# Normed tiles behind norms 2, 3 and 5 one by one from tiles without factor and shift; stacks issued in the norm; last FFN's remainders on VectorE

## Chip, core and metric

One core of one Trainium2 chip runs the whole program. The metric is the device time in microseconds (us), the median of several runs. Engines by their short names: PE (TensorE), DVE (VectorE), ACT (ScalarE), POOL (GpSimd), SP (SyncE, here only a DMA queue).

## What is computed

512 tokens of width 1024, in float32, pass two blocks. Cut to its skeleton:

```python
# block 1
h = rms_norm(x, g_mix);  proj = h @ w_in          # RG-LRU and pooling branches, gates
x = x + merged @ w_out
h = rms_norm(x, g_ffn);  up = conv3(h @ w_up)     # norm 2
x = x + (gelu(up[:, :DF]) * up[:, DF:]) @ w_down
x = rms_norm(x, g_final)                          # norm "g"
# block 2; scale, shift and gate come from mod = silu(c) @ w_mod + b_mod
u = rms_norm(x, g1) * (1 + scale1) + shift1       # norm 3
xs, q, ckv, qi, ki, wi, ga, gb = split(u @ w_in)
y_ssm = s5(xs)                                    # state space branch
y_att = attention(top-128 of causal keys) @ w_attn_proj
x = x + gate1 * ((sig(ga) * y_ssm + sig(gb) * y_att) @ w_out)
u2 = rms_norm(x, g2) * (1 + scale2) + shift2      # norm 5
x = x + gate2 * ((silu(u2 @ w_gate) * (u2 @ w_up)) @ w_down)
return rms_norm(x, final_g)                       # norm 6
```

## The kernel before

**Layout.** Activations lie transposed: eight tiles of 128 channels by 512 tokens. A product of such a tile with weights is a row of "blocks", one block for each 128 by 128 piece of the weights, into one PSUM bank of eight. There are 1976 blocks, in a fixed order; eight blocks are a "unit" of 512 KB.

**Three matmuls a block.** Weights and activations are split into a rounded half (`hi`, fp32r) and a remainder (`lo`). `block` issues hi x hi (L702), lo x hi (L703) and hi x lo (L705), each 512 columns wide. A unit's way: SP loads it (L2435, four buffers `raw`), ACT rounds it (L1115, `whi`), and the remainder `wlo` comes either from ACT (L1124, the negative rounded copy) and a POOL DMA that adds `raw` to it (L2321), or, for the units in `BY_VECTOR`, from a DVE subtraction (L2068). Each stage has four buffers; unit u+4 can be rounded only when PE has done unit u, and loaded only when `wlo` of unit u is there. `weights(n)` in each engine's program moves a counter of blocks and does the units that come due, in that engine's order.

**Norms.** The squares are summed on PE (`sums`, one-column matmuls, L746), ACT takes the root, DVE the inverse, PE spreads it over 128 rows (`to_rows`, L790). DVE multiplies each tile by gain and factor (`nf`, L1556), ACT rounds it and adds the shift (L1151 or L1292), DVE makes the remainder (L1561 or L1544). `first` interleaves the next four tiles, block by block, so that each new normed tile feeds four blocks. Norm 2 already has its first four tiles from x times gain without the factor (`v2`), and DVE multiplies their results by the factor later (L2020). Norms 3 and 5 don't: PE finishes w_down or w_out_2, runs matmuls on unused data (`keep_warm`, L769), and waits for the normed tiles. Squares are summed in two parts there (tiles 0 to 6, and 7).

**Between norm 3 and norm 5** each engine is a set of generators: `d` (attention: index scores, top-128, softmax by pairs of heads), `s` (state space), `g` (gate products), `u` (GLU), `a` (attention projection). One string, `ORDER`, says whose next step follows, and all five engines walk the same string. A step of `g`, `u` or `a` is two blocks on PE. In `d`, a pair of heads has four steps of scores (tokens 3, 2, 1, 0 in quarters; L1004 on PE, DVE's minimum L2212, ACT's exponential L1424, and after the last DVE's reciprocal L2222 and product L2227), two of turning the probabilities (L1019), and one of the product with the values (L1029). `u` on DVE multiplies (L2252) and makes `mod_step`s (L1973): a row of w_mod times the condition, one column of scale, shift or gate each. PLACES gives the steps of `s` (inputs, turn, scan, output, each for four parts).

**Constants of the state space** are made during the first FFN: `CONSTS` says behind which j DVE makes them, `TURNS` behind which j PE turns them (L843) or makes the taps from them (L855), and SP stores them.

Of the kernel before, what the change touches and what calls it, by code (L numbers as in the profile page):

```python
# [319 lines left out]
def layout(k):  # L320
# [159 lines left out]
    for n in ("ssm_b", "ssm_c", "trig", "sbp", "sbt", "scs", "scp", "stt"):  # L480
        give(n)
    run([("uk",)], 2)
    for q in range(4):
        for n in TABS:
            run([(n, q)], TABS[n][1] // S)
# [183 lines left out]
def tensor_engine(k, T):  # L669
# [159 lines left out]
    for m in range(8):  # L829
        tile("w_out", m, range(8), "mg1", [2] if m == 7 else ())  # L830
# [3 lines left out]
    first(FIRST_UP, "v2", {(0, 3): lambda: sums([2], 7), (1, 3): lambda: to_rows(2)})  # L834
# [269 lines left out]
def scalar_engine(k, A):  # L1104
# [183 lines left out]
    root(2, 1024)
    weights(8)
    for m in range(8):  # L1290
        A.wait_ge(at("nf", 2, m), *freed("h2", m, "hi"))
# [1508 lines left out]
```

## Time and profile before

| | |
|---|---|
| median of 3 runs | 1485.59 us (1484.46 to 1486.53) |
| profiled execution | 1487.89 us, span 1486.6 us |
| mean granted clock of PE | 0.997 of full speed |
| PE busy | 98%, 6968 matmul records |
| DVE, ACT, POOL busy | 53%, 56%, 15% |
| DMA | 305.83 MB, mean 206 GB/s |
| to landing (median): raw, wlo, mod | 5.4, 6.3, 8.3 us |

A busy PE says little: the records of matmuls in a row overlap, so the table has 98% also where PE is not at its pace. What counts is the distance from one start to the next. Shares of DVE and ACT are averages over stages of very different load.

### The profile page before, as it was taken

To read this page: it belongs to the slowest core of one execution; us is meant where nothing else is said; L and a number is where in the kernel's file an instruction comes from. 1 tells how busy PE (TensorE), PEld (TensorE's weight loads), DVE (VectorE), ACT (ScalarE), POOL (GpSimd) and SP (SyncE) were. 2 spreads that over 40 slices of the span, in tenths; PEclk is the share of its full clock that TensorE was granted. 3 is DMA by queue.
4 is the path that set the end of the run, shared out by engine and by line. 5 is a ranking of instruction groups with operands and counts; after the bars stand their busy time and mean duration, and the time that the engine had idled before them with its cause. 6 is when DMAs were issued, how large, how long until landed. Compare 5 with 4: busy or idle time off the path is not lost.

```text
span 1486.6 us, 18211 instructions
## 1 busy us (share of the span) xinstructions
PE 1461.1 (98%) x6968; PEld 1191.0 (80%) x6968; DVE 783.0 (53%) x1463; ACT 836.7 (56%) x1122; POOL 222.9 (15%) x241
## 2 busy tenths in 40 slices
PE   9999999999999999999999999999989999999998
PEld 8887888888878778788878877776868888888886
DVE  7879754365595947465346678736663121110011
ACT  7698998755565646542333565686345444444441
POOL 1111111111111111100001421111111111111111
PEclk9999999999999999999999999999999999999999
DMA  9776887899999888783337667894677998888882
GB/s 267 193 188 169 200 200 190 212 322 309 248 265 265 224 207 217 186 267 123 108 105 274 204 171 172 205 277 161 197 192 201 251 218 202 184 190 197 198 184 85
DMA packets 94134, 305.83 MB, mean 206 GB/s; under 512 B 10896, under 2 KB 13200, under 8 KB 94048
## 3 DMA queue, kind: packets, MB, share of 16 engines
q0 software_dynamic: 29696, 108.08, 38.8%
q1 hardware_dynamic: 61104, 190.69, 37.4%
q10 hardware_dynamic: 3248, 5.90, 1.1%
q8 instruction: 55, 0.90, 0.2%
q14 instruction: 31, 0.25, 0.0%
HBM read 177.62 MB, written 17.83 MB: 131 GB/s over the span
## 4 chain that ended last, share of the span: by engine, by line
PE 84%; DVE 8%; ACT 4%; DMA 2%; issue 1%; POOL 0%; DVEq 0%; ACTq 0%
PE ps L702 26%; PE ps L705 26%; PE ps L703 26%; DMA tab<-pl_f 1%; DVE pl_f L1973 1%; PE ps L746 1%; ACT whi L1115 1%; PE ps L790 1%; DVE pl_r L1544 1%; ACT wlo L1124 1%; PE ps L1029 1%; DVE pl_f L2030 1%; DVE pl_f L2027 1%; PE ps L908 0%; ACT pl_f L1231 0%
## 5 line engine op out<-in xcount | busy, mean ns | idle before, releaser
L702 PE MATMUL ps<-pl_r,whi 128*128 128x512 f32 x1976 | 776.5, 393 | 9.4 <-DMA wlo<-raw 3.1
L705 PE MATMUL ps<-pl_r,whi 128*128 128x512 f32 x1976 | 770.2, 390 | 0.0
L703 PE MATMUL ps<-pl_r,wlo 128*128 128x512 f32 x1976 | 769.6, 389 | 0.0
L702 PEld LDWEIGHTS ps<-pl_r,whi 128*128 128x128 f32 x1976 | 371.2, 188 | 95.8 <-issue 12.5
L705 PEld LDWEIGHTS ps<-pl_r,whi 128*128 128x128 f32 x1976 | 371.2, 188 | 79.2 <-DVE pl_r L1561 0.9
L703 PEld LDWEIGHTS ps<-pl_r,wlo 128*128 128x128 f32 x1976 | 371.5, 188 | 75.8 <-issue 0.5
L1115 ACT ACTIVATE whi<-raw 128x1024 fp32r<-128x1024 f32 x246 | 259.1, 1053 | 191.3 <-PE ps L705 153.4
L2321 POOL DMA_DIRECT2D wlo<-raw x206 | 177.7, 864 | 969.2 <-ACT wlo L1124 946.6
L1124 ACT ACTIVATE wlo<-raw 128x1024 fp32r<-128x1024 f32 x206 | 215.4, 1046 | 0.0
L2293 DVE TENSOR_TENSOR pl_f<-ps,pl_f 128x512 f32<-128x512 f32 x22 | 15.2, 691 | 170.6 <-PE ps L705 170.6
L1544 DVE TENSOR_TENSOR pl_r<-pl_f,pl_r 128x512 fp32r<-128x512 f32 x112 | 77.5, 692 | 31.2 <-ACT pl_r L1144 21.7
L2068 DVE TENSOR_TENSOR wlo<-raw,whi 128x1024 fp32r<-128x1024 f32 x39 | 51.4, 1328 | 50.7 <-ACT whi L1115 50.6
L1144 ACT ACTIVATE pl_r<-pl_f 128x512 fp32r<-128x512 f32 x34 | 21.5, 632 | 92.0 <-DVE pl_f L2293 77.0
L2270 DVE SCALAR_TENSOR_TENSOR pl_f<-ps,sml,pl_f 128x512 f32<-128x512 f32 x16 | 12.0, 749 | 116.3 <-PE ps L705 116.3
L1303 ACT ACTIVATE pl_f<-ps,vec 128x512 f32<-128x512 f32 x44 | 33.9, 775 | 55.1 <-PE ps L705 53.3
L1134 ACT ACTIVATE pl_f<-pl_f 128x512 f32<-128x512 f32 x37 | 22.9, 627 | 69.7 <-DVE pl_f L2270 49.8
L1973 DVE CUSTOM_DVE_ANT_0 pl_f<-pl_f,pl_f 128x1024 f32<-128x1024 f32 x48 | 57.9, 1218 | 0.0
L2027 DVE SCALAR_TENSOR_TENSOR pl_f<-ps,vec,pl_f 128x511 f32<-128x511 f32 x44 | 32.7, 744 | 13.2 <-ACT pl_f L1303 13.1
L1497 ACT ACTIVATE pl_f<-ps 128x512 f32<-128x512 f32 x22 | 13.1, 597 | 41.3 <-PE ps L705 41.3
L2030 DVE SCALAR_TENSOR_TENSOR pl_f<-ps,vec,pl_f 128x511 f32<-128x511 f32 x44 | 33.0, 750 | 1.6
L1680 DVE SCALAR_TENSOR_TENSOR pl_f<-pl_f,pl_f 128x512 f32<-128x512 f32 x20 | 12.9, 689 | 34.4 <-ACT pl_f L1243 34.4
L1914 DVE TENSOR_TENSOR pl_f<-pl_f,lams 128x640 f32<-128x640 f32 x4 | 3.3, 826 | 51.3 <-DMA tab<-pl_f 51.3
(270 smaller groups left out, 1095.2 us busy)
## 6 DMA issues: line engine op xcount, KB each, us to landing
raw<-in_w SPq DMA_DIRECT2D x245, 512.0 KB, 5.4
wlo<-raw POOLq DMA_DIRECT2D x206, 512.0 KB, 6.3
pl_f<-in_mod SPq DMA_DIRECT2D x48, 512.0 KB, 8.3
pl_f<-tab SPq DMA_DIRECT2D x12, 512.0 KB, 5.6
xs<-pl_f SPq DMA_DIRECT2D x16, 256.0 KB, 6.1
tab<-pl_f SPq DMA_DIRECT2D x8, 512.0 KB, 6.7
pl_f<-xs SPq DMA_DIRECT2D x16, 256.0 KB, 5.3
spill<-pl_f ACTq DMA_DIRECT2D x16, 256.0 KB, 3.5
```

What stands on the lines that cost most here:

```text
L702: matmul(out, wh, sr(pair, kk, "hi"), start=start, stop=False)
L703: matmul(out, wl, sr(pair, kk, "hi"), start=False, stop=False)
L705: mm = matmul(out, wh, sr(pair, kk, "lo"), start=False, stop=stop)
L1115: act(k.whi[:, u % NHI, :], k.raw[:, u % NRAW, :], ACT.Copy).then_inc(*k.w_hi.tick(("w_hi", u)))
L1124: act(k.wlo[:, u % NLO, :], k.raw[:, u % NRAW, :], ACT.Copy, scale=-1.0).then_inc(*k.w_neg.tick(("w_neg", u)))
L1303: act(sb("up", j), ps("w_up", j), ACT.Identity, bias=vc("conv_f_b", j), scale=vc("conv_f_w", 44 + j)).then_inc(*done.tick(("up_tap", j)))
L1544: tt(sr(pair, m, "lo"), src, sr(pair, m, "hi").bitcast(F32), ALU.subtract).then_inc(*done.tick((pair, m, "lo"), *freed_by))
L1973: V.eng.tensor_tensor_reduce(r, r, sb(*c), 1.0, 0.0, ALU.mult, ALU.add, sm("mod", u)).then_inc(*done.tick(("mod_used", u), *([mod_home(u)] ...
L2027: stt(f[:, 1:S], b[:, 0:S - 1], vc("conv_f_w", j), f[:, 1:S], ALU.mult, ALU.add).then_inc(*done.tick())
L2030: stt(f[:, 0:S - 1], b[:, 1:S], vc("conv_f_w", 88 + j), f[:, 0:S - 1], ALU.mult, ALU.add).then_inc(*done.tick(("up", j), ("w_up", j)))
L2068: tt(k.wlo[:, u % NLO, :], k.raw[:, u % NRAW, :], k.whi[:, u % NHI, :].bitcast(F32), ALU.subtract).then_inc(*done.tick(("w_lo", u)))
L2321: P.eng.dma_start(k.wlo[:, u % NLO, :].bitcast(F32), k.raw[:, u % NRAW, :], accum_op=ALU.add).then_inc(*k.w_lo[u % NLO].tick(("w_lo", u)))
```

## The change

1. **Norms 3 and 5** get what norm 2 has: `v3` and `v5`, tiles of x times gain without factor and shift, feed the first four tiles. The factor is multiplied in afterwards (`scaled`), and the shift, which passes through the weights, is added as a column for each tile: DVE sums the raw weights times the shift (`shift_part`, 8 operations of 128 columns for each of the units 133 to 136 and 181 to 184), PE sums over the rows (`shift_cols`), and ACT adds the column as a bias. SP must wait for `shift_used` before it loads over these units.
2. **The first four tiles** behind norms 2, 3 and 5 come one by one (`in_turn`), not interleaved. The squares are summed once (`sums_once`), and ACT copies the factor's rows to SBUF (`row`). keep_warm goes from norms 3 and 5. w_out_2 interleaves two tiles, not four.
3. **Remainders**: units 138 and 139 move from DVE to ACT and POOL; 185 and 188 to 246 (the last FFN) move from ACT and POOL to DVE (`subtracted`).
4. **Mod steps**: 13 in `u`, not 4; 3 ahead of w_out_2, none in it (12 before). SP's loads of them move with them.
5. **TURNS**: the taps of parts 0, 1 and 2 move from j = 8, 14, 20 to 9, 15, 21.
6. **ORDER and PLACES** are new. SP issues the copies that stack xs (L2580) for parts 1 and 2 in the norm, not at the steps of `s`.

```diff
-BY_VECTOR = [*range(115, 146), *range(169, 177)]
+BY_VECTOR = [*range(115, 138), *range(140, 146), *range(169, 177), 185, *range(188, NUNIT)]
 ORDER = (
-    "dsgggsggsgsgdgsdgggsggdgsgsgdsdgssssgdggggggggdsgddgggggsgdgdgsugdgggddgggdsdduuuduggduddg"
-    "gdgdgggggddudgggdgdgduugdgggugdugdguduuudddduuuudddduuaudduduuuudduddddduuuddddaaaaagauaaa"
+    "dgsgsggssgsgdggdsgdggdgggsgsgsgsgssddgsgggsggggdgudsgggdsgdggdgugddggdguggdddugugduggugdg"
+    "gdgdgddgggdsgggguddgddddggggugdguuduuudddduddduuuudduuuddddduuuuauddudddudduuddddagaauaaaaaa"
     "auaaaaa"
 )
-PLACES = [("b", 0), ("t", 0), ("c", 0), ("b", 1), ("t", 1), ("b", 2), ("t", 2), ("o", 0),
-          ("c", 2), ("c", 1), ("b", 3), ("t", 3), ("c", 3), ("o", 1), ("o", 2), ("o", 3)]
+PLACES = [("b", 0), ("t", 0), ("c", 0), ("b", 1), ("t", 1), ("o", 0), ("b", 2), ("c", 1),
+          ("t", 2), ("c", 2), ("b", 3), ("o", 1), ("t", 3), ("c", 3), ("o", 2), ("o", 3)]
-TURNS = {6: ("b", 0), 8: ("c", 0), 12: ("b", 1), 14: ("c", 1), 18: ("b", 2), 20: ("c", 2),
+TURNS = {6: ("b", 0), 9: ("c", 0), 12: ("b", 1), 15: ("c", 1), 18: ("b", 2), 21: ("c", 2),
...
@@ tensor_engine @@
+    def in_turn(tiles, pair, between):
+        for n, t in enumerate(tiles):
+            out = take(*t)
+            for kk in range(8):
+                block(t, kk, pair, out, kk == 0, kk == 7)
+                for step in between.get((n, kk), ()):
+                    step()
...
-    keep_warm(480, 256)
-    sums([3, "g"], 7)
-    keep_warm(256)
-    to_rows(3)
-    keep_warm(480, 256)
-    first(FIRST_IN_2, "u")
-    to_rows("g")
+    in_turn(FIRST_IN_2, "v3", {(0, 6): [lambda: sums_once(3, "g")],
+                               (1, 2): [lambda: to_rows(3), lambda: shift_cols(0), lambda: to_rows("g")]})
...
-    first([("w_out_2", m) for m in range(4)], "mg2")
+    first([("w_out_2", m) for m in range(2)], "mg2")
...
+    in_turn(FIRST_FFN_2, "v5", {(0, 7): [lambda: sums_once(5)],
+                                (1, 3): [lambda: to_rows(5), lambda: shift_cols(1)]})
@@ scalar_engine @@
+    def normed(n, pair, shift=None, between={}):
+        weights(16)
+        A.wait_ge(at("rows", n), *freed("row", n))
+        act(sb("row", n), ps("rows", n), ACT.Copy).then_inc(*done.tick(("row", n), ("rows", n)))
...
     root(5, 1024)
+    weights(8)
+    rounded_weights(units.ahead())
     normed(5, "h5", lambda m: sm("mod", 24 + m))
@@ vector_engine @@
+    def shift_part(i, part):
+        u = SHIFT_UNITS[4 * i + part]
+        r = sb("shift", i)[:, 128 * part:128 * part + 128]
+        V.wait_ge(at("raw", u))
+        for q in range(8):
+            col, raw = sm("mod", 24 * i + q), k.raw[:, u % NRAW, 128 * q:128 * q + 128]
...
-            if m > 3:
-                mod_step()
+            mod_step((0, 0, 1, 2, 3, 2, 3, 2)[m])
...
     inverse(5)
+    subtracted(185)
...
     for j in range(22):
+        if j > 2:
+            subtracted(184 + 2 * j)
...
+        if j == 1:
+            subtracted(188)
+        elif j > 1:
+            subtracted(185 + 2 * j)
         rest("act2", j, sb("f2", j), ("f2", j))
@@ sync_engine @@
+            if u - NRAW in SHIFT_UNITS:
+                Q.wait_ge(at("shift_used", u - NRAW))
...
-    weights(32)
-
+    weights(24)
     stack(0)
+    weights(8)
+    stack(1)
+    stack(2)
```

## Rows read from the trace of the kernel before

**Rows 1.** The page's busy time of each engine, with its share of the span.
```profile
PE 1461.1 (98%) x6968; PEld 1191.0 (80%) x6968; DVE 783.0 (53%) x1463; ACT 836.7 (56%) x1122; POOL 222.9 (15%) x241
```

**Rows 2.** PE in order of time, w_down: start, length, line, tiles [idle before].
```profile
754.51 0.39 PE L703 MATMUL ps<-pl_r,wlo 128*128 128x512 f32 x1
754.74 0.39 PE L705 MATMUL ps<-pl_r,whi 128*128 128x512 f32 x1
```

**Rows 3.** PE in order of time, in w_out and in the first FFN.
```profile
379.11 0.95 PE L746 MATMUL ps<-cst,pl_f 128*128 128x1 f32 x8
...
428.39 0.47 PE L702 MATMUL ps<-pl_r,whi 128*128 128x512 f32 x1 [1.93 <-DVE pl_f L1872]
```

**Rows 4.** DVE's groups by line and shape: busy us, mean ns | idle before.
```profile
L1544 DVE TENSOR_TENSOR pl_r<-pl_f,pl_r 128x512 fp32r<-128x512 f32 x112 | 77.5, 692 | 31.2 <-ACT pl_r L1144 21.7 <-ACT pl_r L1292 6.3 <-ACT pl_r L1193 0.8
...
L2068 DVE TENSOR_TENSOR wlo<-raw,whi 128x1024 fp32r<-128x1024 f32 x39 | 51.4, 1328 | 50.7 <-ACT whi L1115 50.6
...
L1556 DVE SCALAR_TENSOR_TENSOR pl_f<-pl_f,sml,ps 128x512 f32<-128x512 f32 x16 | 11.9, 743 | 3.3 <-PE ps L790 3.3
...
L1942 DVE TENSOR_TENSOR pl_f<-pl_f,sml 128x128 f32<-128x128 f32 x4 | 1.2, 293 | 0.1
```

**Rows 5.** PE's waits by line: us in total, times, longest.
```profile
PE ps L855 <- DVE pl_f L1922: 3.3, 3, 1.8
```

**Rows 6.** PE in order of time, norm 3.
```profile
754.97 1.84 PE L746 MATMUL ps<-cst,pl_f 128*128 128x1 f32 x16
756.67 0.49 PE L702 MATMUL ps<-pl_r,whi 128*128 128x512 f32 x1
...
788.59 1.05 PE L790 MATMUL ps<-cst,sml 128*128 128x128 f32 x8
789.40 0.48 PE L702 MATMUL ps<-pl_r,whi 128*128 128x512 f32 x1
```

**Rows 7.** Stretches: length, busy time (records) of five engines, PE clock, DMA share, GB/s.
```profile
754.97:789.40 34.43, 33.50 (x158) 26.39 (x157) 17.97 (x26) 13.20 (x20) 0.00 (x0) 0.95 0.35 124
...
1027.60:1030.90 3.30, 3.30 (x10) 2.53 (x9) 1.34 (x9) 3.28 (x13) 0.00 (x0) 0.50 0.33 120
```

**Rows 8.** PE in order of time, w_out_2 and norm 5.
```profile
1099.57 0.47 PE L702 MATMUL ps<-pl_r,whi 128*128 128x512 f32 x1 [1.48 <-DMA wlo<-raw]
...
1104.22 0.39 PE L705 MATMUL ps<-pl_r,whi 128*128 128x512 f32 x1
...
1114.49 0.47 PE L702 MATMUL ps<-pl_r,whi 128*128 128x512 f32 x1 [0.52 <-ACT pl_r L1151]
```

**Rows 9.** POOL and SP's queue in order of time, w_out_2.
```profile
1095.02 0.86 POOL L2321 DMA_DIRECT2D wlo<-raw  x1 [15.43 <-ACT wlo L1124]
...
1099.45 9.66 SPq L2435 DMA_DIRECT2D raw<-in_w  x3
```

**Rows 10.** DVE and POOL in order of time, a step of `u`.
```profile
1002.76 1.22 DVE L1973 CUSTOM_DVE_ANT_0 pl_f<-pl_f,pl_f 128x1024 f32<-128x1024 f32 x1
...
1003.92 2.29 DVE L2068 TENSOR_TENSOR wlo<-raw,whi 128x1024 fp32r<-128x1024 f32 x1
...
1002.94 2.18 POOL L2406 TENSOR_TENSOR pl_f<-pl_f,pl_f 128x512 f32<-128x512 f32 x1 [8.58 <-DVE pl_f L2252]
```

**Rows 11.** PE, ACT and DVE in order of time, heads 2 and 3 (pair 1).
```profile
984.92 2.43 PE L1004 MATMUL ps<-pl_f,pl_f 64*128 64x512 f32 x16
...
995.24 0.82 PE L1019 MATMUL ps<-cst,pl_f 128*128 128x128 f32 x3 [0.38 <-ACT pl_f L1461]
...
990.81 0.39 ACT L1424 ACTIVATE pl_f<-pl_f,sml 128x128 f32<-128x128 f32 x1
...
991.63 2.46 DVE L2227 TENSOR_SCALAR pl_f<-pl_f,sml 128x128 f32<-128x128 f32 x8
```

**Rows 12.** PE in order of time, behind the scores of pair 3.
```profile
1026.90 0.47 PE L702 MATMUL ps<-pl_r,whi 128*128 128x512 f32 x1 [0.69 <-DVE sml L2212]
...
1030.36 0.63 PE L702 MATMUL ps<-pl_r,whi 128*128 128x512 f32 x1
```

More of the change, by code:

```diff
@@ L475, in layout @@
     for m in range(8):
+        if m == 5:
+            for n in ("ssm_b", "ssm_c", "trig", "sbp", "sbt", "scs", "scp", "stt"):
+                give(n)
+            for q in range(8):
+                pair("v3", q)
+            take("shift", 0)
         squares("g", m)
@@ L479, in layout @@
         give_pair("act1", j)
[L480 to L485, printed above, removed]
+    for n in TABS:
+        run([(n, 0)], TABS[n][1] // S)
     give("sq", "g", 0)
@@ L492, in layout @@
         take("st", q)
+    give("shift", 0)
+    run([("uk",)], 2)
+    for n in TABS:
+        run([(n, 1)], TABS[n][1] // S)
+    for m in range(8):
+        give_pair("v3", m)
+    give("row", 3)
+    for q in range(2, 4):
+        for n in TABS:
+            run([(n, q)], TABS[n][1] // S)
     for m in range(8):
@@ L644, in layout @@
     assert not [c for c in "dsgau" if next(steps[c], "end") != "end"]
+    take("shift", 1)
+    for m in range(8):
+        pair("v5", m)
     for m in range(8):
@@ L650, in layout @@
     normed(5, "h5")
+    for m in range(8):
+        give_pair("v5", m)
+    give("row", 5)
+    give("shift", 1)
     for j in range(22):
@@ L761, in sums_of, with shift_cols, sums_once @@
         give("sums", n)
+    def shift_cols(i):
+        b = take("shift_cols", i)
+        T.wait_ge(at("shift_sum", i))
+        for n in range(4):
+            mm = matmul(b[:, n:n + 1], sb("shift", i)[:, 128 * n:128 * n + 128], k.ones[:, 0:1],
+                        start=n == 0, stop=n == 3)
+        mm.then_inc(*done.tick(("shift_cols", i), ("shift", i)))
+        give("shift_cols", i)
+    def sums_once(*norms):
+        b = take("sums", norms[0])
+        for i, n in enumerate(norms):
+            T.wait_ge(at("sq_part", n, 0))
+            for t in range(4):
+                mm = matmul(b[:, 4 * i + t:4 * i + t + 1], sb("sq", n, 0)[:, 128 * t:128 * t + 128],
+                            k.ones[:, 0:1], start=i == t == 0, stop=(i, t) == (len(norms) - 1, 3))
+            mm.then_inc(*done.tick(("sums", norms[0]) if n == norms[-1] else None, ("sq", n, 0)))
+        give("sums", norms[0])
     def keep_warm(*widths):
@@ L829, in tensor_engine @@
     for m in range(8):
[L830 removed]
+        tile("w_out", m, range(8), "mg1")
     done.release(*[("mg1", i, h) for i in range(8) for h in ("hi", "lo")])
[L834 removed]
+    in_turn(FIRST_UP, "v2", {(0, 5): [lambda: sums_once(2)], (1, 2): [lambda: to_rows(2)]})
     done.release(*[("v2", i, h) for i in range(8) for h in ("hi", "lo")])
@@ L1284, in scalar_engine @@
             *done.tick(("v2", m, "hi")))
+    root(2, 1024)
     rounded_weights(units.ahead())
[L1288 to L1291, printed above, removed]
-        act(sr("h2", m, "hi"), sb("nf", 2, m), ACT.Copy).then_inc(*done.tick(("h2", m, "hi")))
-        if m % 2:
-            weights(4)
-    A.wait_ge(at("rows", 2), *freed("row", 2))
-    act(sb("row", 2), ps("rows", 2), ACT.Copy).then_inc(*done.tick(("row", 2)))
-    weights(8)
+    normed(2, "h2")
     def up(j):
@@ L1551, in halves, with normed, factored @@
         rest(pair, m, src, *freed_by)
-    def normed(n, pair, xname, made, gain, shift=None):
+    def normed(n, pair, xname, made, gain, shift=None, between={}):
+        def factored(m):
+            V.wait_ge(at("row", n), at(*made, m), *freed("nf", n, m))
+            stt(sb("nf", n, m), sb(xname, m), gain(m), sb("row", n), ALU.mult,
+                ALU.mult).then_inc(*done.tick(("nf", n, m)))
+        factored(0)
         for m in range(8):
-            V.wait_ge(at("rows", n), at(*made, m), *freed("nf", n, m))
-            stt(sb("nf", n, m), sb(xname, m), gain(m), ps("rows", n), ALU.mult,
-                ALU.mult).then_inc(
-                    *done.tick(("nf", n, m), *([("rows", n)] if m == 7 and n != 2 else [])))
+            if m < 7:
+                factored(m + 1)
             if shift:
@@ L2059, in vector_engine, with subtracted @@
     units.blocks = BLK_DOWN
+    def subtracted(u):
+        V.wait_ge(at("w_hi", u))
+        if u - NLO not in BY_VECTOR:
+            V.wait_ge(at("unit", u - NLO))
+        tt(k.wlo[:, u % NLO, :], k.raw[:, u % NRAW, :], k.whi[:, u % NHI, :].bitcast(F32),
+           ALU.subtract).then_inc(*done.tick(("w_lo", u)))
     def weights(n):
@@ L2588, in s5 @@
         for step, q in PLACES:
-            if step == "b" and q < 3:
-                stack(q + 1)
+            if (step, q) == ("b", 0):
+                stack(3)
             if step == "t" and q in (0, 1):
```

229 lines of the change are left out of this document (145 added, 84 removed).

## The prediction, made before the change was run

> **What bounds the kernel now.** I read the page's busy line first. PE is busy 98% of the span [rows 1], but busy time says little here, as the records of neighbouring matmuls overlap. So I went to PE's own order of time. Two neighbouring starts in a plain stretch lie 0.23 us apart (754.51, 754.74) [rows 2]; that is the pace of a block's three matmuls, 0.68 us a block. The 5928 block matmuls at this pace are 1344 us of the 1486.6. The chip is bound by PE's stream, and a change is worth what it takes out of that stream (small matmuls, waits) less what it puts in. Work of DVE, ACT, POOL or the queues counts only where PE comes to wait for it. So I looked for PE's breaks near each edit, then for what each edit makes late.
>
> **Norm 2.** (T is the end of PE's w_out, and in norms 3 and 5 that of w_down and w_out_2.) One of two groups of eight one-column matmul records goes: 0.95 us of records at 379.11 [rows 3], of which the last overlaps the next block, so 0.8 us of PE's time. DVE now multiplies by a copy of the factor made by ACT, which comes behind ACT's weights(16), so its start slips from T+7.3 to about T+10; eight tiles of two DVE operations (0.74 and 0.69 to 0.75) [rows 4] are 12 us, with 2.8 us of scaling between them. They end near T+25; PE has done the four tiles at 32 x 0.68 + 1.6 = 23.4 and needs the eighth h2 at T+28. Hidden, with 3 us of cover. Behind it PE loses 1.9 us at 428.39 [rows 3], named after DVE, though ACT and the raw loads had fallen behind. DVE's scaling ends some 2 us earlier than before, and SP's loads with it: between nothing and the whole 1.9 comes back; I take 1.0, the middle.
>
> **TURNS.** The small tap matmuls (L855) of the first three parts go one j later, 16 blocks or 10.9 us. The three waits there sum to 3.3 us [rows 5], none over 1.8, so all go: 3.3 us. Below, SP's store of tt moves too and could hold raw loads (gain 0). The store waited for PE's turn before as well, so I take 3.3.
>
> **Norm 3.** From the first small matmul at 754.97 to the block behind the "g" rows at 789.40 are 34.4 us [rows 6, 7]. In it lie 99 matmuls of blocks, 22.4 us. What else must stay: the sums once, 754.97 to 756.67, 1.7; rows 3 and rows g, each 788.59 to 789.40, 0.8; and, new, shift_cols, eight one-column records as at 379.11, 0.8 [rows 3, 6]. Sum 22.4 + 1.7 + 0.8 + 0.8 + 0.8 = 26.5: 7.9 us less. Will it be covered? w_down ends at T; DVE adds the last tile to 1.7 (it first has w_lo 134 and 135, 1.3 us each [rows 4]), squares, makes v3 7 by 3.3, adds both sums by 4.7; PE asks for them at 7 x 0.68 = 4.8. A tie, 0.1 us. The normed u takes 12 us plus 2.5 of scaling from T+11 plus about 2 behind ACT's weights: T+28. PE asks for u 7 at 26.5 + 4.8 = T+31. The 32 DVE operations of shift_part(0) (128 columns; 0.29 us for the nearest such row [rows 4]) are 9 us in the last w_down tiles, where DVE has 15 us a tile. SP's new wait for shift_used has only raw loads behind it, and comes after w_lo of the same unit, which they waited for anyway: nothing. Stacks on SP: stack 1 and 2 wait for ACT's xs 2 near T+28 with the next raw loads behind them; those feed PE only at T+58. Nothing. I take 7.8.
>
> **Norm 5.** 1104.45 to 1114.49 holds one block and 9.4 us else [rows 8]: a wait for DVE's gain2, keep-warm, sums, rows. Kept: sums, rows, new shift_cols, 3 x 0.8 = 2.4. So 7.0 less. The wait before it for w_lo (1.48, 1099.57) came from ACT standing behind DVE's mod steps; these are moved, so 1.5 less. New: ACT makes unit 183 only after the root, and PE needs it 16 blocks and 2.4 us behind T, at 13.3. ACT has it at 8.7; its DMA took 4.4 us from 1095.02 to SP's next load at 1099.45 [rows 9], so 13.3 at best; one of 6.3 (the page's median) makes PE wait 1.9. h5 7, behind unit 185 on DVE, comes near 29.5, wanted at 29. I take 0.8 for both: 7.7 gained; bounds 4 and 8.5. That the shared work of DVE and POOL grows could cost more: a subtraction next to a POOL tensor operation took 2.29 us, against 1.33 in the mean of all 39 [rows 4, 10]. [...]
>
> **Last FFN.** 60 subtractions of 1.3 us [rows 4] go to DVE, which has 5.3 us of work in each 10.9 us pair of tiles. subtracted(185+2j) stands behind f2 j, which waits for PE; it is needed 10.9 us after that and done 2.3 us after. Cover 8.6 us. PE is at its pace there now, so freeing ACT and the POOL queue gives nothing: 0. If the cover failed, each of 60 units would cost.
>
> **ORDER.** This decides. Each letter takes a generator one step, so I laid both strings against the steps of the generators ("d": 27 steps, then for each pair of heads four scores, two turns, one product; "g", "u" and "a" put two blocks each, 1.36 us, between). The old string gives PE's order as the trace has it, to the block: in pair 1 four scores, "uuuu", both turns. The new one has 58 "d" for 55 steps, and those of pairs 1 to 3 stand where the spare ones have pushed them. Pair 0 keeps twelve blocks between scores and turns. Pair 1 has "ddd" (scores 3, 2, 1), "u", "ddd" (score 0 and both turns). Pair 2 has score 3, "uuu", "ddddd" (scores 2, 1, 0 and both turns). Pair 3 has score 3, "u", "ddd" (scores 2, 1, 0), "u", "dd" (both turns). A turn (L1019) needs all four queries' parts: DVE's minimum, ACT's exponentials, DVE's reciprocal and product. For pair 1 now: scores from 984.92, the last exponential over at 991.2, products 991.63 to 994.1 [rows 11]. That is 9.2 us from the first score. Before, 24 block matmuls stood in it. Now the scores (2.4) and two blocks (1.4) do: the 20 turn records (2.1) would be done at 5.9 and are at 9.7. Stall 3.8 us. Pair 2: from score 2, pair 1's 9.2 less the two widest exponentials, 1.7, plus another table load for the sigmoid between, 1.3: 8.8, and some 0.6 for DVE's three mod steps (1.22 each) [rows 10] and its subtraction; without waiting 3.5. Stall 5.9. Pair 3: u6.3 puts a multiply and three mod steps, 4.4 us, on DVE between score 3 and score 2; chain 11 against 4.9. Stall 6.1. Together 15.8 us. PE idles 4 to 6 us three times. The granted clock was 0.95 in norm 3, where PE stood, instead of 1.00, and 0.50, 1.2 GHz, behind the waits that end at 1026.90, where a block's record took 0.63 us, not 0.39 [rows 2, 7, 12]. That lasted 3.4 us and cost 1.5. Two or three of those: 3.8. By the Trainium skill, "TensorE: Matmul & The Clock Gate", section "What's actually happening", an idle stretch brings the half clock and activity releases it; here that would be three, 4.5, where the rows alone leave two open. Against this the waits of the old order in pairs 1 to 3 go, as those at 995.24 and 1026.90: by the starts of PE's records, against the same records unhindered, 1.8, 1.4 and 1.3 us, and the half clock's 1.5 [rows 11, 12], some 6.0. Net 15.8 + 3.8 - 6.0 = +13.6. Bounds: 0 (DVE and ACT turn out to be early enough and the old waits stay) to +27 (each chain 3 us longer, by subtractions of 2.29). I take 13.6.
>
> **Sum.** -0.8 - 1.0 - 3.3 - 7.8 - 7.7 + 13.6 = -7.0. The profiled execution took 1487.9 us (span 1486.6, 1.3 around it); its successor should take 1480.9. The median of the runs is 2.3 lower than the profiled one, so 1478.5.
>
> **Rivals.** (A) The turns do not stall: another reading of ORDER, or chains that are shorter without the work between. For it: ACT and DVE are less loaded there than PE. Against: the two chains that I followed took 9.2 us (pair 1, from the first score) and 7.4 (pair 2, from the last score). Then -20.6: 1465. Chance 0.22. (B) The norms' streams starve: DVE makes remainders, squares and normed tiles in turn with ACT, and PE, that now comes without a pause, waits for v3, unit 183, u and h5, 2 us at each of three places: 1484.5. For it are the tie at T+4.8 and the h5 of 29.5 against 29. Chance 0.14. (C) Slower: the softmax chains of pairs 1 to 3 grow. It decides when they lose more than 20.6 net, that is 9 us each with a half clock behind each (27 + 4.5 - 6 = 25.5 net, 1490.5). The place is DVE in pairs 2 and 3, with three mod steps and subtractions of 2.29. Chance 0.11. (D) The parts cancel and nothing is to be seen, 1485.6: 0.06. The forecast has 0.47, and its own range is 1473 to 1483.
>
> **How the numbers follow.** 0.2% is 3 us, about what a measurement of this kernel can tell from no change. Faster: A, nearly all of the forecast, a third of B, 0.73. Same: two thirds of B and D, 0.14. Slower: C and bits, 0.13. The range leaves out C's upper half and the end of A: 1463 to 1488.
>
> **What would show it.** PE's order of time: blocks without a break from w_down into w_in_2 and from w_out_2 into the FFN, no keep-warm, about 26.5 us for the same norm 3 work; no L855 wait; then at the turns of pairs 1, 2 and 3 waits for DVE's product of 3 to 6 us each, with the granted clock low behind them. No such waits, and I am wrong by 13 us on the fast side. A wait for w_lo 12 to 15 us after w_out_2 would be unit 183. Waits in the last FFN, at any j, would mean that DVE has no cover.

## The result, and where the time went

The changed kernel took 1470.32 us (median of 4 runs, 1467.47 to 1471.86) against 1486.06 of the kernel before (4 runs, 1484.46 to 1490.65). The ratio is 0.9877, with a 95% interval of 0.9861 to 0.9894. That is 15.7 us less; the prediction had 7.0 less (1478.5, range 1463 to 1488). The profiled execution took 1471.86 us, its span 1470.2 against 1486.6.

First a mistake that the reader must know of. The ORDER quoted above in the diff, and laid out in the prediction, is miscopied. The first line of it lacks one "g" (behind "ssdd" comes "gsgggg", not "gsggg"), which shifts nothing in the attention. The second has two "d" too many. These are the two lines of the kernel that ran:

```
"dgsgsggssgsgdggdsgdggdgggsgsgsgsgssddgsggggsggggdgudsgggdsgdggdgugddggdguggdddugugduggugdg"
"gdgdgddgggdsgggguddgddddggggugdguuduuudduddduuuudduuuddddduuuuauddudddudduuddddagaauaaaaaa"
```

They hold 56 "d", not 58. Laid against the generators again they give pair 1 score 3, two blocks, scores 2, 1 and 0, eight blocks, both turns; pair 2 four scores, twelve blocks, both turns; pair 3 scores 3 and 2, two blocks, scores 1 and 0, four blocks, both turns. So each chain keeps four to twelve blocks of cover, where the prediction had none or two.

The busy line and two groups of the page after (cf. [rows 1, 4]): POOL's DMAs finish 148 remainders, DVE makes 97.

```profile
PE 1450.7 (99%) x6932; PEld 1188.3 (81%) x6932; DVE 886.9 (60%) x1613; ACT 787.0 (54%) x1080; POOL 173.6 (12%) x183
...
L2461 POOL DMA_DIRECT2D wlo<-raw x148 | 127.9, 864 | 839.1 <-ACT wlo L1173 698.4
L2162 DVE TENSOR_TENSOR wlo<-raw,whi 128x1024 fp32r<-128x1024 f32 x97 | 120.1, 1242 | 93.0 <-ACT whi L1164 92.9
```

PE's blocks are the same 1976 in both kernels, so I counted the first matmul of each block (L702 before, L725 after) and took the differences of their starts. Each stretch begins and ends at such a start:

| stretch (blocks) | before | after | difference | forecast |
|---|---|---|---|---|
| start to w_out (to 520) | 368.91 | 371.82 | +2.9 | 0 |
| w_out, norm 2, its stall (520 to 600) | 59.48 | 56.28 | -3.2 | -1.8 |
| rest of the first FFN (600 to 1050) | 317.73 | 317.29 | -0.4 | -3.3 |
| norm 3 (1050 to 1100) | 46.11 | 38.56 | -7.6 | -7.8 |
| gated part, attention (1100 to 1430) | 298.89 | 298.17 | -0.7 | +13.6 |
| w_out_2, norm 5 (1430 to 1500) | 59.10 | 51.69 | -7.4 | -7.7 |
| last FFN (1500 to 1975) | 323.81 | 323.81 | 0.0 | 0 |

The differences sum to -16.4, as the spans do. The largest miss by far is in one row, the attention's. No run below takes the edits of norms 2, 3 and 5 out again: those rows rest on the same blocks timed in both kernels.

**Norm 3**, PE in order of time; it answers to [rows 6].

```profile
759.67 1.84 PE L813 MATMUL ps<-cst,pl_f 128*128 128x1 f32 x16
...
764.23 1.05 PE L845 MATMUL ps<-cst,sml 128*128 128x128 f32 x8
765.12 0.95 PE L802 MATMUL ps<-cst,pl_f 128*128 128x1 f32 x8
765.94 1.14 PE L845 MATMUL ps<-cst,sml 128*128 128x128 f32 x8
766.83 0.48 PE L725 MATMUL ps<-pl_r,whi 128*128 128x512 f32 x1
...
786.67 0.39 PE L725 MATMUL ps<-pl_r,whi 128*128 128x512 f32 x1
```

The sums of both norms stand once between blocks. Rows 3, shift_cols and rows g stand together, 764.23 to 766.83. The window from the first sum to the block behind the same 33 blocks, with the columns of [rows 7]:

```profile
759.67:786.67 27.00, 27.00 (x141) 23.07 (x139) 20.92 (x34) 14.88 (x22) 1.72 (x2) 1.00 0.72 213
```

It is 27.0 us against the 34.4 of [rows 7] and the 26.5 of the forecast; the granted clock is 1.00 in it, where it was 0.95.

**Norm 5**: PE in order of time, cf. [rows 8].

```profile
1099.92 0.50 PE L725 MATMUL ps<-pl_r,whi 128*128 128x512 f32 x1 [0.64 <-ACT pl_r L1197]
...
1101.05 0.95 PE L813 MATMUL ps<-cst,pl_f 128*128 128x1 f32 x8
```

PE waits 0.64 us for the v5 that ACT makes from the last tile. Nothing else ends a wait here, unit 183 and h5 included: in place of 9.4 us there are the sums, the rows and shift_cols, and this wait.

**Attention**: PE in order of time, scores (L1056) and turns (L1071) of pairs 1, 2 and 3, cf. [rows 11, 12].

```profile
973.40 1.13 PE L1056 MATMUL ps<-pl_f,pl_f 64*128 64x512 f32 x4
...
976.05 1.57 PE L1056 MATMUL ps<-pl_f,pl_f 64*128 64x384 f32 x12
...
984.03 3.07 PE L1071 MATMUL ps<-cst,pl_f 128*128 128x128 f32 x20 [0.74 <-DVE pl_f L2348]
...
993.43 3.30 PE L1056 MATMUL ps<-pl_f,pl_f 64*128 64x512 f32 x16
...
1005.57 3.06 PE L1071 MATMUL ps<-cst,pl_f 128*128 128x128 f32 x20 [0.44 <-DVE pl_f L2348]
...
1012.25 1.77 PE L1056 MATMUL ps<-pl_f,pl_f 64*128 64x512 f32 x8
...
1017.17 2.21 PE L1056 MATMUL ps<-pl_f,pl_f 64*128 64x256 f32 x8 [1.55 <-DVE pl_r L1614]
```

Turn waits of 0.74 and 0.44 us, none at pair 3. The largest loss is a new one: score 1 of pair 3 waits 1.55 us, and a stretch at 1.2 GHz stands behind it (granted clock 0.50 from 1019.3 to 1022.4).

**First FFN**: the stall of [rows 3] at 428.39 is gone and so are the three waits of [rows 5], but a new stall stands at 503.21: PE, then the window behind it.

```profile
503.21 0.47 PE L725 MATMUL ps<-pl_r,whi 128*128 128x512 f32 x1 [2.06 <-DVE pl_f L2127]
...
505.00 0.63 PE L728 MATMUL ps<-pl_r,whi 128*128 128x512 f32 x1
```

```profile
503.70:507.00 3.30, 3.30 (x9) 2.61 (x9) 3.23 (x5) 3.13 (x10) 0.86 (x1) 0.51 1.06 235
```

The page names DVE L2127 for this wait, but DVE's operation is due on each tile. What was late is a unit's weights: SP's queue, then ACT.

```profile
472.88 0.33 SPq L2577 DMA_DIRECT2D raw<-in_w  x1
473.30 0.91 SPq L2648 DMA_DIRECT2D tab<-pl_f  x1
491.70 0.33 SPq L2625 DMA_DIRECT2D pl_f<-in_mod  x1
492.13 11.30 SPq L2577 DMA_DIRECT2D raw<-in_w  x4
```

```profile
499.29 1.06 ACT L1164 ACTIVATE whi<-raw 128x1024 fp32r<-128x1024 f32 x1 [5.49 <-DMA raw<-in_w]
```

SP is through with a store at 474.2. Its next instruction is the load of modulation weights (`mod`, L2625), which must wait until DVE has used an older tile; it goes at 491.70. Four raw loads stand behind it in the program. ACT, which makes whi from them, stands still for 5.49 us until 499.29. The stall is 2.2 us by the starts and the half clock (0.51) costs 1.4 more: what TURNS gave is gone again.

The hold is not new. In the kernel before the same load goes at 490.37, behind a store of 473.11, and PE waits 0.50 us at the same block. Counted from block 600 it goes 62.0 us on there and 63.6 in the changed kernel. What delays it by 1.6 us is not shown; with the same code it varies, as E1 shows.

### The profile page after: what moved, and what is told of

Same layout as the page of the kernel before. It is cut to its first block, busy times and chain, and to the rows that moved or that the text cites. A ratio compares the mean times of both kernels' runs of the same rounds, so it can differ in the third digit from the quotient of the medians.

```text
span 1470.2 us, 18182 instructions
## 1 busy us (share of the span) xinstructions
PE 1450.7 (99%) x6932; PEld 1188.3 (81%) x6932; DVE 886.9 (60%) x1613; ACT 787.0 (54%) x1080; POOL 173.6 (12%) x183
## 4 chain that ended last, share of the span: by engine, by line
PE 86%; DVE 5%; ACT 5%; DMA 2%; issue 1%; POOL 0%; DVEq 0%; ACTq 0%
PE ps L725 27%; PE ps L728 27%; PE ps L726 27%; DVE pl_f L2050 1%; DMA wlo<-raw 1%; ACT whi L1164 1%; ACT wlo L1173 1%; ACT pl_f L1287 1%; PE ps L1071 1%; PE ps L845 1%; DMA tab<-pl_f 1%; PE ps L960 0%; PE ps L979 0%; DVE pl_f L2073 0%; PE ps L834 0%
## 5 line engine op out<-in xcount | busy, mean ns | idle before, releaser
L725 PE MATMUL ps<-pl_r,whi 128*128 128x512 f32 x1976 | 777.5, 393 | 8.4 <-DMA wlo<-raw 2.7
L725 PEld LDWEIGHTS ps<-pl_r,whi 128*128 128x128 f32 x1976 | 372.2, 188 | 91.9 <-issue 8.8
L2461 POOL DMA_DIRECT2D wlo<-raw x148 | 127.9, 864 | 839.1 <-ACT wlo L1173 698.4
L2162 DVE TENSOR_TENSOR wlo<-raw,whi 128x1024 fp32r<-128x1024 f32 x97 | 120.1, 1242 | 93.0 <-ACT whi L1164 92.9
L1173 ACT ACTIVATE wlo<-raw 128x1024 fp32r<-128x1024 f32 x148 | 154.8, 1046 | 0.0
L2050 DVE CUSTOM_DVE_ANT_0 pl_f<-pl_f,pl_f 128x1024 f32<-128x1024 f32 x48 | 63.1, 1331 | 3.8 <-ACT pl_f L1325 3.8
L1599 DVE TENSOR_TENSOR pl_f<-pl_f,pl_f 128x512 f32<-128x512 f32 x34 | 23.6, 693 | 19.8 <-ACT pl_f L1183 19.0
L2127 DVE SCALAR_TENSOR_TENSOR pl_f<-ps,vec,pl_f 128x511 f32<-128x511 f32 x44 | 33.0, 750 | 1.5
L1757 DVE SCALAR_TENSOR_TENSOR pl_f<-pl_f,pl_f 128x512 f32<-128x512 f32 x20 | 12.9, 689 | 34.4 <-ACT pl_f L1299 34.4
```

The source lines that it names most:

```text
L725: matmul(out, wh, sr(pair, kk, "hi"), start=start, stop=False)
L1173: act(k.wlo[:, u % NLO, :], k.raw[:, u % NRAW, :], ACT.Copy, scale=-1.0).then_inc(*k.w_neg.tick(("w_neg", u)))
L2050: V.eng.tensor_tensor_reduce(r, r, sb(*c), 1.0, 0.0, ALU.mult, ALU.add, sm("mod", u)).then_inc(*done.tick(("mod_used", u), *([mod_home(u)] ...
L2127: stt(f[:, 0:S - 1], b[:, 1:S], vc("conv_f_w", 88 + j), f[:, 0:S - 1], ALU.mult, ALU.add).then_inc(*done.tick(("up", j), ("w_up", j)))
L2162: tt(k.wlo[:, u % NLO, :], k.raw[:, u % NRAW, :], k.whi[:, u % NHI, :].bitcast(F32), ALU.subtract).then_inc(*done.tick(("w_lo", u)))
L2461: P.eng.dma_start(k.wlo[:, u % NLO, :].bitcast(F32), k.raw[:, u % NRAW, :], accum_op=ALU.add).then_inc(*k.w_lo[u % NLO].tick(("w_lo", u)))
```

## The experiments

All times are medians. The kernel before, timed beside each group of experiments, stood at 1488.3 (E1 to E4), 1487.9 (E5 to E8), 1489.0 (E9 and E10) and 1488.9 us (E11), so ratios say more than times. Differences between kernels of under 3 us are not settled by either; for them the text goes by the stretches, and each stretch is of one execution. Stretches are by counted blocks, as above.

**E1, the changed kernel again.**

> The changed kernel once more, unchanged. In the profiled execution of it the first 32 block matmul groups start 2.7 us later, against the kernel before, than they should with the same code, and the loss stays. Theory: this differs from execution to execution (a wait and a stretch of 1.2 GHz at 19 to 25 us), so here it can be gone or of another size, and the time is 1470 give or take 3. Rival: it belongs to the changed kernel (its constants, its loads); then the same wait of 1.8 us at 19.4 stands here too, and in each of the kernels below, whose first 300 us are the same.

Measured: 1468.85 us (4 runs, 1465.99 to 1473.80), ratio 0.9877 [0.9855, 0.9899]. Block 32 starts at 32.67 us, as in the kernel before (32.86), not at 35.57. Over the twelve profiled executions of this study's kernels it starts between 32.6 and 35.6, with the same code. So the +2.9 of the table is the execution, not the kernel. The stall at 500 differs in the same way: here it is 0.5 us, without a half clock (blocks 600 to 900: 209.96 us, in the first execution 213.57); the held load goes 61.3 us behind block 600, not 63.6. Behind block 950 the two executions agree to 0.2 us.

**E2, the order as the prediction read it.**

```diff
-... "ggggugdguuduuudduddduuuudduuuddddd" ...
+... "ggggugdguuduuudddduddduuuudduuuddddd" ...
```

> The changed kernel with the order as the prediction read it: two more d behind the 130th letter, so that scores and softmax turns of pairs 1 to 3 stand as close as the prediction had them. Theory (the prices of the step were right, only the string was misread): waits of about 3.8, 5.9 and 6.1 us at the turns of pairs 1, 2 and 3 and 3.8 us of 1.2 GHz, together 19.6, where the changed kernel has about 5.5 of such losses: 14 us above it, 1484. Rival (DVE and ACT catch up while PE stands, so that the chains are shorter than summed): 1.5 to 3 us at each turn, 3 to 6 us above it, 1473 to 1476.

Measured: 1486.52 us (10 runs), ratio 0.9993 [0.9981, 1.0004]: 17.7 us above the changed kernel (E1), where the theory had 14 and the rival 3 to 6, and all the gain is gone. PE at pairs 1 to 3:

```profile
972.77 2.25 PE L1056 MATMUL ps<-pl_f,pl_f 64*128 64x512 f32 x12
976.53 0.49 PE L1056 MATMUL ps<-pl_f,pl_f 64*128 64x128 f32 x4
...
981.36 4.33 PE L1071 MATMUL ps<-cst,pl_f 128*128 128x128 f32 x20 [4.34 <-DVE pl_f L2348]
...
993.42 1.13 PE L1056 MATMUL ps<-pl_f,pl_f 64*128 64x512 f32 x4
...
998.78 1.57 PE L1056 MATMUL ps<-pl_f,pl_f 64*128 64x384 f32 x12
...
1006.90 4.78 PE L1071 MATMUL ps<-cst,pl_f 128*128 128x128 f32 x20 [6.56 <-DVE pl_f L2348]
...
1022.49 1.13 PE L1056 MATMUL ps<-pl_f,pl_f 64*128 64x512 f32 x4
...
1025.13 1.57 PE L1056 MATMUL ps<-pl_f,pl_f 64*128 64x384 f32 x12
...
1032.24 0.77 PE L725 MATMUL ps<-pl_r,whi 128*128 128x512 f32 x1 [5.54 <-DVE sml L2333]
...
1035.96 4.23 PE L1071 MATMUL ps<-cst,pl_f 128*128 128x128 f32 x19 [0.82 <-DVE pl_f L2348]
```

The turns of pair 1 wait 4.34 us (forecast 3.8), those of pair 2 6.56 (5.9); in pair 3 the block ahead of the turns waits 5.54 and they another 0.82, 6.4 together (6.1). The granted clock is 0.50 at all three: from 981.7 to 985.1, 1005.6 to 1012.4 and 1029.5 to 1039.7. The stretch from block 1100 to 1400 takes 295.15 us, 16.7 more than before; the forecast for it was +13.6. It is 17.4 more than in the changed kernel, and PE's waits (17.3 and 2.9 us) explain 14.4 of that. The other 3.0 and the 1.5 that the half clock costs the changed kernel make an estimate of 4.5 us for the half clock here, where the step had 3.8. DVE in pair 2:

```profile
996.84 1.22 DVE L2050 CUSTOM_DVE_ANT_0 pl_f<-pl_f,pl_f 128x1024 f32<-128x1024 f32 x1
...
997.98 2.30 DVE L2050 CUSTOM_DVE_ANT_0 pl_f<-pl_f,pl_f 128x1024 f32<-128x1024 f32 x1
...
1001.35 1.21 DVE L2162 TENSOR_TENSOR wlo<-raw,whi 128x1024 fp32r<-128x1024 f32 x1
...
1006.47 2.46 DVE L2348 TENSOR_SCALAR pl_f<-pl_f,sml 128x128 f32<-128x128 f32 x8
```

Three mod steps and a subtraction, 996.84 to 1002.5, stand between the minima of score 3 and those of score 2; only then come the other minima, exponentials, reciprocal and the products at 1006.47. The turns start at 1006.90, while the products still run. So the stalls are what the prediction made them, to 0.7 us; it is the string that was read wrongly. The agreement is in part luck. Counted to the end of the products the chains are longer than it had them (pair 2 from score 2: 998.78 to 1008.93, 10.2 us for 9.4), and the turns do not wait for that end.

**E3, ORDER and PLACES of the kernel before.**

```diff
-    "dgsgsggssgsgdggdsg" ... (ORDER and PLACES as changed)
+    "dsgggsggsgsgdgsdgg" ... (ORDER and PLACES as before)
```

> The changed kernel with ORDER and PLACES of the kernel before. Theory: the two orders cost the same within a microsecond (by the starts of the block matmuls the attention stage took 0.7 us less in the changed kernel), 1471. Rival: the new order pays for what the new norm 3 makes late (stacks, u, table loads); with the old one PE waits in the first 100 us behind norm 3, some 3 to 6 us, 1474 to 1476.

Measured: 1473.56 us, ratio 0.9903 [0.9887, 0.992], 3 to 5 us above the changed kernel. The theory falls by the time and the rival by the place. No new wait stands behind norm 3: blocks 1100 to 1250 take the 137.7 us that they took before (the new order 136.0). The loss comes later, in the attention.

```profile
985.33 3.08 PE L1071 MATMUL ps<-cst,pl_f 128*128 128x128 f32 x20 [1.07 <-DVE pl_f L2348]
...
1008.50 3.06 PE L1071 MATMUL ps<-cst,pl_f 128*128 128x128 f32 x20 [1.87 <-DVE pl_f L2348]
...
1020.08 1.09 PE L1056 MATMUL ps<-pl_f,pl_f 64*128 64x128 f32 x4 [2.71 <-DVE pl_r L1614]
...
1021.87 0.49 PE L725 MATMUL ps<-pl_r,whi 128*128 128x512 f32 x1 [0.69 <-DVE sml L2333]
```

Waits of 1.07, 1.87, 2.71 and 0.69 us: blocks 1100 to 1400 take 282.17 us, with the new order 277.77, in the kernel before 278.49. So beside the other edits the old order is 3.7 us dearer than it was, and the new one takes 4.4 off.

**E4, SP's loads of modulation weights later.**

```diff
-        if 2 <= j < 8:
+        if 3 <= j < 9:
             load_mod()
```

> The changed kernel with SP's six loads of modulation weights in the first FFN one j later (3 <= j < 9 instead of 2 <= j < 8). In the changed kernel PE waits 2.2 us at 500.8 and runs 1.6 us long at 1.2 GHz behind it; the last of those loads stood in SP's queue from 474 to 491.7 until DVE had used an older tile, with four raw loads behind it. Theory: the raw loads come about 10 us earlier and the whole goes, 3.8 us below the changed kernel, 1466.5. Rival (the raw loads are late because the transfers themselves are slow there, or DVE's own work is what PE waits for): the wait stays, same time.

Measured: 1467.25 us, ratio 0.9865 [0.985, 0.988]. Blocks 600 to 900 take 209.16 us; seven executions with the loads in their old place and the new TURNS lie between 209.96 and 215.12, mean 212.9. SP's queue:

```profile
469.65 0.42 SPq L2625 DMA_DIRECT2D pl_f<-in_mod  x1
476.80 5.50 SPq L2577 DMA_DIRECT2D raw<-in_w  x2
488.86 0.33 SPq L2625 DMA_DIRECT2D pl_f<-in_mod  x1
492.38 5.41 SPq L2577 DMA_DIRECT2D raw<-in_w  x2
```

Two raw loads now go at 476.80; counted from the same block that is 13 us earlier than in the changed kernel, and the stall is gone, here as in the other three kernels with the later loads (E8, E10, E11). The last load still waits, until 488.86, but less stands behind it. The median is 1.6 to 3.1 us below the changed kernel's and the intervals overlap, so the whole 3.8 of the theory is not shown. In this execution 1.5 us went at pair 3, where the half clock lasted longer, and 1.5 in norm 5, where there was none before.

**E5, TURNS as before, and E11, the same with the loads of E4.**

```diff
-TURNS = {6: ("b", 0), 9: ("c", 0), 12: ("b", 1), 15: ("c", 1), 18: ("b", 2), 21: ("c", 2),
+TURNS = {6: ("b", 0), 8: ("c", 0), 12: ("b", 1), 14: ("c", 1), 18: ("b", 2), 20: ("c", 2),
```

> The changed kernel with the tap turns of the first three parts at j of 8, 14 and 20 again (TURNS as before). Theory (the prediction's step on TURNS): the three waits for the taps in the first FFN come back, 3.3 us by the waits, at least 2.4 by the starts of PE's records: from block 600 to block 900, which took 214.0 us in the kernel before and 210.0 and 209.2 us in the two executions of the new order of turns that had no other stall there, 212.5 to 214. Rival: the waits belonged to the late raw loads of SP and not to the place of the turn; then the stretch stays at 209 to 210.

> The changed kernel with TURNS as before and the modulation loads one j later, to price TURNS where the stall at 500 is away. From block 600 to block 900 the three executions with the later loads and the new TURNS took 209.2, 209.9 and 209.2 us. Theory (TURNS is worth its waits, and the stall at 500 had taken them back): the waits for the taps return and the stretch takes 2.4 to 3.3 us more, 212 to 212.5. Rival (TURNS is worth nothing by itself; the later loads did it all): 209 to 210.

Measured: E5 1469.87 us, ratio 0.9882 [0.9857, 0.9906]; blocks 600 to 900 212.35 us. PE's waits by line:

```profile
PE ps L910 <- DVE pl_f L1999: 2.7, 2, 2.3
```

So the waits for the taps do come back, 2.7 us, but the stretch is within what the changed kernel shows, as the stall at 500 isn't there in this execution. E11, 1469.69 us, ratio 0.9865 [0.9837, 0.9894]: waits of 1.6 us, and 210.91 us against 209.2 to 209.9 of E4, E8 and E10. That is less than the theory's 2.4 to 3.3 and more than the rival's nothing. TURNS is worth some 1 to 1.7 us where nothing else is late, by one execution against three, and nothing measurable in the changed kernel as it stands.

**E6, the last FFN's remainders back on ACT and POOL.**

```diff
-BY_VECTOR = [*range(115, 138), *range(140, 146), *range(169, 177), 185, *range(188, NUNIT)]
+BY_VECTOR = [*range(115, 138), *range(140, 146), *range(169, 177), 185]
...
     def subtracted(u):
+        if u not in BY_VECTOR:
+            return
```

> The changed kernel with the remainders of the units from 188 on back on ScalarE and GpSimd's accumulating DMA; units 183 to 187 as in the changed kernel. Theory (the prediction's step on the last FFN, priced at nothing): PE's starts in the last FFN are the same to 0.1 us, the time within run noise of the changed kernel, 1470. Rival: the relief of ACT and of the POOL queue at the head of the FFN is part of what was booked on norm 5: then block 1430 to 1500, 51.7 us in the changed kernel against 59.1 before, grows by 1 to 2 us.

Measured: 1470.6 us, ratio 0.9886 [0.9866, 0.9907]. Blocks 1500 to 1975 take 323.81 us and blocks 1430 to 1500 51.69, to the hundredth what they took. The move costs nothing and brings nothing.

**E7, the mod steps spread.**

```diff
-            mod_step((0, 0, 1, 2, 3, 2, 3, 2)[m])
+            mod_step((0, 0, 2, 2, 2, 2, 2, 3)[m])
```

> The changed kernel with DVE's 13 modulation steps of the gated part spread (0, 0, 2, 2, 2, 2, 2, 3) instead of (0, 0, 1, 2, 3, 2, 3, 2): one less ahead of the scores of pair 2 and of pair 3. The order of before put into the changed kernel lost 10 us where the kernel before lost 6, and one difference between the two in that stage is these 13 steps, so I expect them to be what lengthens the softmax chains. Theory: the wait of 1.5 us before the last scores (score 1 of pair 3) and the 1.5 us of 1.2 GHz behind it go, each shorter chain 1.2 us early: 2.5 to 3.5 us below the changed kernel in the stretch from block 1300 to 1370. Rival: PE waits there for another member of the chain (ACT's exponentials, the product's remainder) and the stretch of 83.5 us stays within 0.5.

Measured: 1466.42 us, ratio 0.9866 [0.984, 0.9893]. Blocks 1300 to 1370 take 81.54 us, 1.9 less than 83.46 (the changed kernel and E1, E4, E5, E6 and E11, which share its order and steps, lie between 83.45 and 84.98). PE at pair 3 and in norm 5:

```profile
1010.71 2.18 PE L1056 MATMUL ps<-pl_f,pl_f 64*128 64x256 f32 x8 [0.40 <-DVE pl_r L1614]
...
1016.55 3.06 PE L1071 MATMUL ps<-cst,pl_f 128*128 128x128 f32 x20 [0.69 <-DVE pl_f L2348]
...
1088.91 0.47 PE L725 MATMUL ps<-pl_r,whi 128*128 128x512 f32 x1 [0.88 <-DVE pl_f L2073]
```

The wait of score 1 fell from 1.55 to 0.40, by about one mod step (1.22), and the half clock is gone, but PE comes earlier to the turns and waits 0.69 there. Less than the theory's 2.5 to 3.5, in the right place. Of the 1.9 us 1.1 go back in blocks 1430 to 1500 (52.81 us for 51.69): PE now waits 0.88 us for DVE at the first block of the FFN. Such a wait stands there in all four kernels with the spread steps (0.5 to 0.9 us, E7 to E10) and in none of the other eight executions of the new code. So it belongs to the edit, which is worth some 0.8 us net; that the mod step moved to the last `u` step makes it is likely and not shown.

**E8, the edits of E4 and E7, and v5 7 ahead of its square in norm 5** (ACT's lines; DVE's likewise).

```diff
+        if m < 7:
             square(5, m, sb("xz", m), ("x", 5, m))
         factorless("v5", m, sb("xz", m), ("x", 5, m), sm("gs2", m), "gain2")
+        if m == 7:
+            square(5, m, sb("xz", m), ("x", 5, m))
...
-    in_turn(FIRST_FFN_2, "v5", {(0, 7): [lambda: sums_once(5)],
-                                (1, 3): [lambda: to_rows(5), lambda: shift_cols(1)]})
+    in_turn(FIRST_FFN_2, "v5", {(1, 1): [lambda: sums_once(5)],
+                                (1, 4): [lambda: to_rows(5), lambda: shift_cols(1)]})
```

> The changed kernel with the spread steps of the run before this, the later loads of the modulation weights in the first FFN, and in norm 5 the last v5 made ahead of its square on ACT and DVE, with the sums two blocks and the rows one block later. Theory: of the changed kernel's losses the stall at 500.8 with its half clock (up to 3.8, absent in some executions), the one at 1015.2 with its half clock (3) and 0.9 of the wait for v5 7 go: 1463 to 1465. Rival: the later sums make h5 late, and PE waits for h5 7 what it saved, 1465 to 1467.

Measured: 1465.39 us (5 runs), ratio 0.9855 [0.9834, 0.9876]. PE in norm 5:

```profile
1094.47 0.50 PE L725 MATMUL ps<-pl_r,whi 128*128 128x512 f32 x1 [0.17 <-ACT pl_r L1197]
...
1105.68 0.47 PE L725 MATMUL ps<-pl_r,whi 128*128 128x512 f32 x1 [1.15 <-DMA wlo<-raw]
```

The wait for v5 fell to 0.17 us, but PE then waits 1.15 us for a remainder that POOL's DMA brings. That is the wait that the prediction feared of unit 183; it comes only when the rest is faster. Blocks 1430 to 1500 take 54.24 us, not 51.69. Of these 2.5 us 1.1 come with the spread steps (E7 and E10 have 52.81); the third edit loses the other 1.4. The two others hold in their own stretches (209.86 and 81.55 us). The time is at the rival's lower end, but h5, on which the rival put it, makes no wait.

**E9, the old order with the steps spread.**

> The changed kernel with ORDER and PLACES of the kernel before, as in e3_order_before, and with the 13 modulation steps spread (0, 0, 2, 2, 2, 2, 2, 3). Theory: what made the old order dearer in the changed kernel (3.7 us from block 1250 to 1400 beyond the kernel before) is the modulation steps that DVE now makes between the chains; with one less ahead of pairs 2 and 3, 2 to 3 us of it come back, 1471. Rival: it is another part of the change in that stage (SP's stacks, the reordered tables), and the stage stays at 282 us from block 1100 to 1400.

Measured: 1474.78 us, ratio 0.9908 [0.9883, 0.9934]. Blocks 1100 to 1400 take 281.06 us against 282.17 in E3; 1300 to 1370 85.09 against 86.22. Of the 3.7 us 1.1 came back, half of what was expected, and all in one wait: that of pair 3's score went from 2.71 to 1.56 us, while the turns of pair 2 still wait 1.86. The median did not fall, as blocks 1430 to 1500 took 54.35 us for 51.59. That the mod step ahead of pair 3 is a part of the cause is shown; that the added steps are all of it is not.

**E10, E4 and E7 together.**

> The changed kernel with the spread modulation steps and the later loads of the modulation weights, and norm 5 as in the changed kernel, since the later sums of e8_together met a wait of 1.3 us for the remainder of unit 183 in its place. Theory: it keeps 1.9 us from the steps and the stall at 500 stays away, 1464 to 1466. Rival: what is gained in single executions is run noise of 2 to 3 us at the start and in the first FFN, and it stands at 1468 as the changed kernel's second timing.

Measured: 1464.73 us (5 runs, 1464.31 to 1468.47), ratio 0.9843 [0.9818, 0.9868]: the fastest kernel of the study. By the two ratios it is 0.34% ahead of the changed kernel (0.9843 against 0.9877), but the intervals overlap; the stretches (209.21 us for blocks 600 to 900, 81.61 for 1300 to 1370) show that both edits hold, and blocks 1430 to 1500 (52.81) that the 1.1 us of E7 is paid here too.

## Why the prediction was wrong

- **ORDER, +13.6, is the step that failed.** It said "The new one has 58 "d" for 55 steps"; the string has 56. The stage came out at -0.7. With the string as read (E2) the three stalls are 4.3, 6.6 and 6.4 us where the step had 3.8, 5.9 and 6.1, and the stage +16.7 where it had +13.6. The rows and the stalls made from them were right to 0.7 us each, the input of the reading was wrong. The profiled executions differ by 16.4 us, 9.4 more than the sum of -7.0; ORDER was 14.3 off to one side, all else together 4.9 to the other. Without the step the sum is -20.6, rival A ("another reading of ORDER", 1465). The measured time lies in the stated range, but by that rival, which had a chance of 0.22, and not by the forecast's working.
- **Rival A gave 4.2 us too much** against the profiled execution: 2.9 of the start, which is the execution's own (E1), 2.9 of TURNS, 0.5 of norms 3 and 5, less 1.4 that norm 2 and 0.7 that the attention gave beyond it. The old order's losses of 6.0 were not saved either; others of nearly their size stand at new places.
- **Norm 3, -7.8: right** (-7.6, the stretch 27.0 us for 26.5). The tie at v3 7 went well: no wait.
- **Norm 5, -7.7: right** (-7.4). The 0.8 booked for unit 183 and h5 fell due elsewhere, as 0.64 for v5 7. POOL's issues took no longer next to more DVE work: 864 ns in mean in both kernels.
- **Norm 2, -0.8, and the stall behind it, -1.0: the first right, the second less than half.** The whole stall went: block 520 to 560 gave 1.0 and 560 to 600 2.2. The value was the middle between nothing and 1.9; all twelve executions with the new code show 56.28.
- **TURNS, -3.3: mechanism right, gain taken back.** Its waits went in the changed kernel and came back in E5 and E11, but units came late behind a held load in SP's queue instead (E4). The prediction asked whether SP's store would hold raw loads; it didn't. A load that was held in the kernel before as well did. E11 prices TURNS at 1 to 1.7.
- **Last FFN, 0: right**, to 0.01 us in E6.
- **Moved mod steps**: the prediction charged them only within the chains of ORDER. E9 shows 1.1 us for the one ahead of pair 3; what the other 2.6 us of the old order's rise are isn't settled.

## What to carry to other kernels

An order written as a string is data: copy it by program and count it against the steps of its generators (here 56 letters for 55 steps and an end) before any time is drawn from it; a count that doesn't fit says that the copy is wrong, not that letters are spare. Price a stall by adding what DVE and ACT do in their own order from the first score on: that came out within 0.7 us three times, with errors that in part cancelled. And a wait taken away on PE is worth its length only if the next unit is there in time, so look at what stands in the load queue behind a load that waits for a buffer, and at where the engine that makes the inputs is when PE comes earlier (E7, E8).

## What the hardware showed

The slow operation beside POOL's multiply is whichever DVE starts second. Before, it was the subtraction [rows 10]; now it is the second mod step, here DVE and then POOL in order of time:

```profile
1000.39 1.22 DVE L2050 CUSTOM_DVE_ANT_0 pl_f<-pl_f,pl_f 128x1024 f32<-128x1024 f32 x1
...
1001.53 2.30 DVE L2050 CUSTOM_DVE_ANT_0 pl_f<-pl_f,pl_f 128x1024 f32<-128x1024 f32 x1
```

```profile
1000.55 2.20 POOL L2546 TENSOR_TENSOR pl_f<-pl_f,pl_f 128x512 f32<-128x512 f32 x1 [8.94 <-DVE pl_f L2373]
```

The first mod step takes 1.22 us, the second, which starts inside POOL's 2.20, takes 2.30: 1.08 more. POOL, which starts 0.16 behind the first step, ends about 1.1 us after that step's end; the same multiply takes 1.29 us where DVE does not run such a pair beside it (at 969.4), so it pays 0.9. Over the whole trace no mod step of 48 took over 1.3 us before, and five took 2.28 to 2.31 after; four subtractions of 39 took 2.1 to 2.3 before, two of 97 took 1.9 and 2.3 after. By the Trainium skill, "SBUF — State Buffer", section "SBUF: two separate sides", VectorE and GpSimd share a pair of ports, which one of the two holds for a whole operation while the other waits; these rows agree, and show 1.08 us on DVE's side and 0.9 on POOL's. Putting another operation second moved the loss and did not save it; a shorter one was not tried.

The half clock (granted clock 0.50, 1.2 GHz) can't be told from the length of the last wait. At block 704 it stood behind waits of 2.0 to 2.4 us in four executions and not behind 2.1 in a fifth (E6). At score 1 of pair 3 a wait of 1.5 us had it from 1019.2 to 1022.6 in the changed kernel and for twice as long in E4, E5 and E11. A wait of 0.40 there was without it in E7 and E8 and had it in E10:

```profile
1011.60:1015.00 3.40, 3.40 (x10) 2.65 (x9) 1.44 (x10) 3.38 (x13) 0.00 (x0) 0.50 0.91 302
```

In norm 5 it stood behind 0.7 us in E4 and E11, and not behind 0.8 in E2. Behind PE's 4.3 us idle in E2 the 20 turn records took 4.33 us, 3.07 in the changed kernel. The stretches at 504 and at 1019 cost 1.4 to 1.5 us each.
